# Order and waits of three experts' weight loads, and two unread products, in a mixture-of-experts layer step

## The reference

```python
def _hier_moe(x, router_group, router_expert, w_gate, w_up, w_down):
    ...
    g_top, g_idx = lax.top_k(g_prob, 1)
    ...
    e_top, e_idx = lax.top_k(e_in_group, TOP_K)
    ...
    hid = jax.nn.silu(jnp.einsum('td,edf->tef', t, w_gate)) * jnp.einsum('td,edf->tef', t, w_up)
    y = jnp.einsum('tef,efd->td', hid * gates[:, :, None], w_down)
```

## Time and profile before

| | us |
|---|---|
| median of 3 runs | 666.19 (664.73 to 667.28) |
| profiled execution, its own time | 668.42 |
| span of the profile, first to last instruction | 666.5 |
| PE busy | 550.8 (83% of the span) |
| DMA engines, mean rate over the span | 260 GB/s |

### The profile page before, as it was taken

How to read it: one execution, slowest core, us unless ns; L and a number is a source line. 1 busy time by engine, 2 the same in 40 slices (tenths; PEclk the granted TensorE clock), 3 DMA queues, 4 the chain that set the end, 5 groups by cost and what they waited for, 6 DMA issues and landing times.

```text
span 666.5 us, 9139 instructions
## 1 busy us (share of the span) xinstructions
PE 550.8 (83%) x3055; PEld 302.9 (45%) x3055; DVE 188.9 (28%) x571; ACT 151.5 (23%) x374; POOL 175.5 (26%) x242
## 2 busy tenths in 40 slices
PE   0569999999987888999997769899999698888700
PEld 0235664444445455455553436465665344444300
DVE  1140132001176665144447401111111111101027
ACT  2620012001106655122222011111111110111133
POOL 1000000001422433133333523334344322231204
PEclk9998999999997999999998889999999988899965
DMA  8999106136099500541159739999999999999368
GB/s 247 405 404 397 77 1 245 71 115 263 1 267 411 207 2 1 186 161 64 64 193 393 256 122 391 409 400 412 404 402 403 391 385 394 411 412 408 128 275 212
DMA packets 53935, 173.15 MB, mean 260 GB/s; under 512 B 7740, under 2 KB 8420, under 8 KB 52976
## 3 DMA queue, kind: packets, MB, share of 16 engines
q1 hardware_dynamic: 45680, 153.88, 60.0%
q0 software_dynamic: 7184, 15.70, 7.2%
q10 hardware_dynamic: 1008, 2.75, 1.0%
HBM read 163.75 MB, written 16.68 MB: 271 GB/s over the span
## 4 chain that ended last, share of the span: by engine, by line
PE 47%; DMA 37%; DVE 6%; ACT 3%; SPq 3%; issue 2%; POOL 1%; POOLq 0%; ACTq 0%; DVEq 0%
DMA ring<-in_w_down_dram 15%; PE ps L719 10%; PE ps L616 10%; PE ps L597 6%; PE ps L518 4%; DMA w_6d<-in_w_down_dram 4%; PE ps L866 4%; DMA ring<-in_w_mod_dram 4%; DMA ring<-in_w_up_dram 4%; DMA w_7d<-in_w_down_dram 3%; PE ps L598 3%; DMA w<-in_w_down_dram 2%; PE ps L696 2%; PE ps L536 2%; PE ps L874 2%
## 5 line engine op out<-in xcount | busy, mean ns | idle before, releaser
L866 PE MATMUL ps<-ring,xt 128*64 128x256 f32 x704 | 88.2, 407 | 12.9 <-DMA ring<-in_w_up_dram 8.0
L866 PEld LDWEIGHTS ps<-ring,xt 128*64 128x64 f32 x704 | 58.0, 146 | 49.1 <-issue 19.1
L616 PE MATMUL ps<-ring,h_t 128*128 128x512 f32 x160 | 69.5, 594 | 0.0
L1359 DVE TENSOR_TENSOR hid<-act_g,ps 128x128 f32<-128x128 f32 x32 | 9.2, 287 | 193.3 <-ACT act_g L1577 193.3
L866 PE MATMUL ps<-w,xt 128*64 128x256 f32 x416 | 49.8, 391 | 8.2 <-DMA w<-in_w_up_dram 5.0
L719 PE MATMUL ps<-ring,mix_t 128*128 128x512 f32 x120 | 53.6, 596 | 0.0
L1703 POOL DMA_INDIRECT expert_results<-y_sb,idx_out x32 | 32.7, 1021 | 57.1 <-ACT y_sb L1591 49.6
L616 PEld LDWEIGHTS ps<-ring,h_t 128*128 128x128 f32 x160 | 30.1, 190 | 37.6 <-issue 37.6
L866 PEld LDWEIGHTS ps<-w,xt 128*64 128x64 f32 x416 | 34.2, 140 | 28.1 <-DMA w<-in_w_up_dram 8.5
L597 PE MATMUL ps<-ring,h_t 128*128 128x512 f32 x80 | 43.1, 622 | 2.7 <-DVE h_t L1018 2.7
L1634 POOL TENSOR_TENSOR gm_stats<-gm_stats,half_pow 128x8 f32<-128x8 f32 x5 | 9.7, 1940 | 132.3 <-DVE gm_stats L1084 132.3
(11 more groups left out here) (239 smaller groups left out, 731.8 us busy)
## 6 DMA issues: line engine op xcount, KB each, us to landing
ring<-in_w_mod_dram SPq DMA_DIRECT2D x8, 3072.0 KB, 19.6
ring<-in_w_gate_dram SPq DMA_DIRECT2D x20, 1024.0 KB
ring<-in_w_up_dram SPq DMA_DIRECT2D x20, 1024.0 KB
ring<-in_w_down_dram SPq DMA_DIRECT2D x20, 1024.0 KB
w<-in_w_gate_dram SPq DMA_DIRECT2D x12, 1024.0 KB
w<-in_w_up_dram SPq DMA_DIRECT2D x12, 1024.0 KB
y_back<-expert_results SPq DMA_DIRECT2D x5, 1024.0 KB, 8.9
ring<-in_w_in_dram SPq DMA_DIRECT2D x2, 2048.0 KB, 17.5
```

Of the source, the lines that this page charges most:

```text
L616: last = pe.matmul(ps[:, 4 + u % 4, :], h_t[:, k, i * P:(i + 1) * P], w[:, k, :], start=(k == 0), stop=(k == KC - 1))
L866: last = pe.matmul(bank[fh * SLOT:(fh + 1) * SLOT, 0:FE].rearrange("p (a f) -> p a f", a=2), x_t[:, k % 4, (k // 4) * SLOT:(k // 4 + 1) * ...
```

## The change

SP's loads between expert 3 and the loop are written in another order and with other waits. Before, three pieces of experts 5 and 4 are issued as soon as the storage under them is free, ahead of the last tile's store and the gathers. After, all three pieces of expert 4 wait until all three first gathers (`xg_in[0]` to `xg_in[2]`) have landed, and experts 5 and both remaining down matrices (5 and 6) wait until the extra tile's gather has landed (`e_in`). The last `keep_warm` has 2 products in place of 4. Nothing else differs.

```diff
             load_expert(RING - 1)
-            sp.wait_ge(res1, 2 * TILES)
-            load_down(5)
             sp.wait_ge(rt_mm, TILES)
             sp.wait_ge(sq3, 2 * TILES)
-            load_down(4)
-            load_half(4, 1)
-
             sp.wait_ge(h2_out[0], 16 * 3)
             sp.wait_ge(h2_out[1], 16 * 2)
-            sp.wait_ge(xg_in[XS - 1], 16)
-            load_half(4, 0)
-            sp.wait_ge(rows_made, MAIN_ROWS)
-            load_half(5, 0)
-            load_half(5, 1)
+            for j in range(XS):
+                sp.wait_ge(xg_in[j], 16)
+            load_expert(4)
             sp.wait_ge(rows_made, ALL_ROWS)
+            sp.wait_ge(e_in, 16)
+            load_expert(5)
             load_down(6)
...
             last.then_inc(r_idx, 1)
-            keep_warm(4)
+            keep_warm(2)
```

## The result

The changed kernel takes 662.85 us (median of 7 runs, 659.92 to 663.37), the kernel before on the same chips 667.28 (664.73 to 668.07). The ratio is 0.9925, 95% interval 0.9908 to 0.9943: 5.0 us faster, between 3.8 and 6.1. Forecast were 5.8 us.

A forecast was written before the change was run, and what follows sets the result against it. The weight stream was taken to bound the kernel, so DMA idle ahead of it counts: 8.8 + 1.6 = 10.4 us against 16.2, 5.8 less, giving 660.4 us from 666.19. Own range 658.5 to 662.3; wider range 657.5 to 664.5.

The forecast's parts named there:

- The bound: Second half of the kernel: a weight stream at about 402 GB/s that ends earlier only if its bytes start earlier.
- The store: Last tile's store, with three weight pieces no longer ahead: 3.0 us in place of 7.67, landing 4.7 us earlier.
- The gathers and products(0): After the last store: gathers 3.85 us earlier, released by DVE's row numbers; clock effects on turns and products(0) taken as 0.
- the 0: Net cost of two unread products dropped before the turns and products(0): taken as 0, bounds +1.0 and -1.3 us.
- Expert 4 and the extra gather: Expert 4's weights issued at 369.2 us; extra gather issued at 377.0, landing at 380.6, when the next four pieces go out.
- The second hole: DMA idle between expert 4's weights and expert 5's: 1.6 us.
- Expert 7: Expert 7's load issued at about 391 us in place of 398.76, with expert 5's landing as the new limit.
- The cover of 2.5 us: Ahead of expert 7: four pieces keep the engines busy to 394.5 us, covering its wait to 391 by some 2.5 us.
- The slow extra gather: Rival: extra gather beside expert 4's weights still takes 6.74 us, landing at 383.75; gain only 2.7 us, 663.5; chance 0.12.
- PE's start as the bound: Rival: the stream starts as early as PE allows, all 8.3 us at expert 7 come through, 657.9 us; chance 0.10.
- The store's rival: Last store slow for another reason or only partly for weights, engines sharing evenly: 663.0 to 664.3 us; chance 0.15.
- The slower case: Held-back weights reopen the second gap: extra gather landing after 386.4 us loses the gain, at 390 gives 669.8; chance 0.07.

The follow-up runs named there:

- the ten kernels of the first table: The kernel before, the changed kernel and eight edited variants of either, timed against the kernel before; ratios from 0.9893 to 1.0001.
- 1 MB more: Changed kernel plus one 1 MB DRAM-to-DRAM copy that nobody reads, issued behind down 6 and ahead of expert 7; ratio 0.9958 to the kernel before.
- the changed kernel's second trace: The changed kernel run once more, unedited, beside two other variants on one chip; ratio 0.9936 to the kernel before.
- the run without the extra wait: Changed kernel without SP's wait for the extra tile's gather, so seven weight pieces go out together behind the first three gathers; ratio 0.9938 to the kernel before.
- the run with all seven pieces behind: Changed kernel with expert 4's three pieces also held until the extra tile's gather has landed; ratio 1.0001 to the kernel before.
- the run with the wait only: Kernel before, with gate and up of expert 5 and down 6 waiting for the extra tile's gather, nothing else changed; ratio 0.9947 to it.

## Why the prediction was right

**The bound.** "It ends earlier only if the bytes start earlier" held in every run. Over the ten kernels of the first table the shift of products(30) follows the idle within 1 us, from -6.3 us at 11.8 to +1.1 at 19.4. 1 MB more is the one exception in kind, since the idle doesn't count the bytes it added: with its idle taken as 12.3 it starts them 0.8 us later than the idle says, the others 0.2 to 0.9 us earlier.

**The store.** 3.0 us, as taken. The first gather released by the row numbers, 3.76 us earlier (predicted 3.85).

**The gathers and products(0).** The extra gather was issued 3.7 us earlier (3.85). The clock did not stay at 1.2 GHz into the turns, as feared. Windows of PE alone, for the turns and for the start of products(0) (busy, clock, DMA share, GB/s):

```profile
364.33:365.78 1.45, 1.45 (x8) 1.00 0.42 113
366.00:369.00 3.00, 3.00 (x14) 0.50 0.40 90
```

The turns ran at 2.4 GHz, 1.45 us against 1.85 before. Then the clock fell, and products(0) took 5.23 us against 4.95. The forecast had slower turns and, if anything, faster products(0); both came out the other way round and all but cancelled. So that the 0 was right to 0.2 us is luck.

**Expert 4 and the extra gather.** SP issued expert 4 at 28.2 behind the anchor, 369.1 on the clock of before (369.2 predicted). The gather landed at 380.7 (380.6), the four pieces went out at 380.8 (380.6). The second hole was 1.9 us (1.6), the first 9.4 (8.8).

**Expert 7.** Here a step was off. It went out at 52.7 behind the anchor, 393.7 on the clock of before, not at 391: the wait for expert 5 was sized at 10.4 us from the first issue and took 12.9 (its last piece, issued 0.9 us behind the first, took 11.94). In the changed kernel's second trace all four pieces have their landing; they were issued within 1.7 us, and these are the issues of the first and the last (KB, us to landing):

```profile
w<-in_w_gate_dram SPq DMA_DIRECT2D x1, 1024.0 KB, 6.8
w_7d<-in_w_down_dram SPq DMA_DIRECT2D x1, 1024.0 KB, 13.6
```

The two between took 9.9 and 11.8. So they land one after the other, as I had let them, but later. What the sum lacked are bytes: from the first issue (378.3) to expert 5's landing (391.1) the engines moved 353 GB/s, 4.5 MB, and expert 5 is 3.1 of them. Two gathers and a scatter, issued at 377.65, 380.02 and 382.61, are 0.8 MB, 2.0 us; I had counted them behind expert 5, for the cover only. What is left, 0.6 MB, must be mostly part of expert 6's down matrix, which was issued right behind. The cover of 2.5 us that stood behind it was just used up: from 391 to 394 the share in single us is 0.96, 0.87 and 0.89, 0.3 us in all. That expert 5 and not expert 0 ends SP's wait, as forecast, costs no more than that yet. PE has expert 0 behind it when it starts the next products, at 390.7 on the clock of before (390.5 predicted).

**The sum.** Forecast 5.8 us; idle 4.7 less, bytes 4.6 us ahead, products(30) 5.6 earlier, the ratio 5.0 (3.8 to 6.1). The terms that were too small are the two holes (together 0.9 us) and the dips in front of expert 7 (0.3). Between the idle's 4.7 and products(30)'s 5.6 lie 0.9 us. 0.4 of them are idle in the stream itself: over the 192 us behind the stretch it is 1.7 us before and 1.3 after (1.1 to 1.4 in every other run), for the same 77.3 MB. The rest stays open.

**The rivals.** The slow extra gather did not come with the change, but the run without the extra wait shows its case: 6.5 us beside weights. PE's start as the bound is refuted by the run with all seven pieces behind. The store's rival was right in one point and I wrong: I held 7.67 us for the time until the weights in front are through, and the third piece landed 2.8 us behind the store (the run with the wait only). The gather that landed at 382.6 with the engines full until 391 shows that a small transfer gets turns between the weights. That is what the Trainium skill, "DMA: Bandwidth & Descriptors", "Queues, rings and completion order", states (each engine takes turns between queue rows, a packet at a time), and this run agrees with it. Even sharing does not follow: the store then should have lost 1.3 us and lost 4.7. How the turns are dealt out is not shown by any run. The conclusion for the store stood, since it rested on the row of 3.0 us and not on how the sharing works.

**The slower case.** A late landing of the extra gather was given as the way to lose, and no run has one. A loss of that size appears another way, when expert 4 is held back with the rest: 6.6 us to the changed kernel, with a gather of 2.90 us.

## What to carry to other kernels

When the second half of a kernel is one stream of bytes, count the idle of the DMA engines ahead of it, in us, for both versions; the difference is the forecast, and what an engine gains beyond it is waited away. Small transfers on which an engine waits want the weights out of their way only where the weights still fit in behind them: none held back cost 17.5 us of idle here, all held back 19.4, the splits in between 11.3 to 13.8. And compare two profiles from an instruction that the change doesn't touch: the same store, behind equal code, started up to 4.6 us apart.

## What was not expected of the hardware

A gather of 64 rows (0.26 MB) landed in 2.90 us without weights beside it, in 3.50 beside their last three us (3.99 in the same kernel's second trace), and in 6.49 and 6.74 beside seven and four pieces of 1 MB: three more pieces in the queue cost it nothing here. The store of 0.5 MB behaved alike, 7.4 us with two late pieces and 7.7 with three. Four pieces of 1 MB issued within 1.7 us landed 6.8, 9.9, 11.8 and 13.6 us after their issues, beside three small transfers. And PE, given half the unread work (3.45 us) and then 1.5 us of rest, turned the rows at a granted clock of 1.00 (2.4 GHz) and then fell to 0.50 (1.2 GHz) for most of the products that followed (5.23 us against 3.67), which here cost nothing.
